# Eight projection products placed singly between the quarters of the scores and of the value pages, from the third sample on

## What is computed

```python
sb = jnp.einsum('bqhjd,bkhjd->bjhqk', qf, kb) - slopes[:, None, None] * d   # scores
pb = jnp.exp(sb - m_new[..., None])
acc = acc * corr[..., None] + jnp.einsum('bjhqk,bkhd->bjhqd', pb, vb)       # values
...
a = o[:, 0] - lam * o[:, 1]
mix = jnp.concatenate([a.reshape(B, S, ATT_W), s_out], axis=-1) @ w_out     # projection
x = x + ga1 * rms_norm(mix, g_post_mix)
```

## Time and profile before

| | us |
|---|---|
| median of 3 runs | 844.1 (839.42 to 849.49) |
| the profiled execution, its own time | 844.71 |
| span of the profile | 842.9 |
| time outside the span | 1.8 |
| mean granted clock of TensorE | 0.948 |

### The profile page before, as it was taken

One profiled execution on the slowest core, in us unless ns is written; L12 is line 12 of the kernel. 1 busy time (PEld: TensorE's weight loads), 2 busy tenths in 40 slices (PEclk: granted clock), 3 DMA queues, 4 the chain that ended last, 5 costly groups with the idle time before them and its releaser, 6 DMA issues.

```text
span 842.9 us, 12264 instructions
## 1 busy us (share of the span) xinstructions
PE 761.0 (90%) x5020; PEld 366.9 (44%) x5020; DVE 361.7 (43%) x830; ACT 184.0 (22%) x426; POOL 116.5 (14%) x169
## 2 busy tenths in 40 slices
PE   4699999999999839999999744999999999999994
PEld 3244343444444524545555333544444444444431
DVE  2212252536798846947665667100131011010146
ACT  4001000124454412413333211011011011110132
POOL 2220000200001111313221200100000000000054
PEclk9899999999999969979899965999999999999997
DMA  8979096580000996999999944788899999999793
GB/s 305 400 229 416 30 393 215 159 300 14 13 2 20 368 403 272 422 384 353 415 376 349 389 194 160 301 342 331 313 408 407 421 397 398 422 386 402 310 310 113
DMA packets 36602, 249.52 MB, mean 296 GB/s; under 512 B 4137, under 2 KB 5417, under 8 KB 23106
## 3 DMA queue, kind: packets, MB, share of 16 engines
q1 hardware_dynamic: 26482, 165.02, 50.5%
q0 software_dynamic: 9120, 81.34, 24.7%
q10 hardware_dynamic: 944, 2.38, 0.7%
HBM read 232.32 MB, written 16.40 MB: 295 GB/s over the span
## 4 chain that ended last, share of the span: by engine, by line
PE 74%; DMA 10%; DVE 9%; issue 2%; POOL 2%; SPq 2%; ACT 1%; POOLq 0%; DVEq 0%; ACTq 0%
PE ps L778 10%; PE ps L2454 8%; PE ps L2464 7%; PE ps L2489 7%; PE ps L1679 6%; PE ps L1069 5%; PE ps L2461 5%; PE ps L1597 4%; DMA sb<-in_w_ada 3%; PE ps L1647 3%; PE ps L2494 2%; DMA sb<-in_w_out 2%; PE ps L2426 2%; PE ps L535 2%; PE ps L1625 2%
## 5 line engine op out<-in xcount | busy, mean ns | idle before, releaser
L2464 PE MATMUL ps<-sb 128*128 128x512 f32 (+1 forms) x256 | 112.9, 594 | 0.0
L778 PE MATMUL ps<-sb 128*128 128x512 f32 x192 | 87.4, 610 | 1.4 <-DVE sb L436 1.4
L2388 DVE TENSOR_TENSOR sb<-sb,ps 128x512 f32<-128x512 f32 (+1 forms) x16 | 10.9, 684 | 160.4 <-PE ps L2464 94.7
L817 DVE STREAM_TRANSPOSE sb<-sb 128x1024 f32<-128x1024 f32 (+1 forms) x72 | 76.5, 1099 | 0.0
L2454 PE MATMUL ps<-sb 128*128 128x512 f32 x144 | 65.5, 608 | 1.0 <-ACT sb L2306 0.9
L2489 PE MATMUL ps<-sb 128*128 128x512 f32 x144 | 63.5, 594 | 0.0
L1679 PE MATMUL ps<-sb 128*128 128x512 f32 x128 | 61.9, 640 | 0.0
L1069 PE MATMUL ps<-sb 128*128 128x512 f32 x128 | 59.2, 597 | 0.3 <-DVE sb L972 0.3
L2464 PEld LDWEIGHTS ps<-sb 128*128 128x128 f32 (+1 forms) x256 | 42.0, 167 | 34.0 <-issue 34.0
L778 PEld LDWEIGHTS ps<-sb 128*128 128x128 f32 x192 | 36.5, 195 | 46.0 <-issue 42.9
L2461 PE MATMUL ps<-sb 128*64 128x512 f32 x112 | 49.6, 595 | 0.0
(11 more groups left out here) (347 smaller groups left out, 993.5 us busy)
## 6 DMA issues: line engine op xcount, KB each, us to landing
sb<-in_w_gate SPq DMA_DIRECT2D x16, 2048.0 KB, 19.0
sb<-in_w_up SPq DMA_DIRECT2D x16, 2048.0 KB, 9.9
sb<-in_w_down SPq DMA_DIRECT2D x16, 2048.0 KB, 14.4
sb<-in_w_ada SPq DMA_DIRECT2D x12, 2048.0 KB, 18.6
sb<-in_w_in SPq DMA_DIRECT2D x5, 2048.0 KB, 27.8
y_rows<-sb SPq DMA_DIRECT2D x9, 512.0 KB, 16.0
sb<-in_x_prompt SPq DMA_DIRECT2D x8, 512.0 KB, 6.7
sb<-in_w_out SPq DMA_DIRECT2D x2, 2048.0 KB, 20.6
```

Of the source, the lines that this page charges most:

```text
L778: last = pe.matmul(PS[:, n % 4, :], L.hT[:, k, t * P:t * P + P], w[:, k, :], start=k == 0, stop=k == KC - 1)
L817: dve.transpose(block, block).then_inc(self.turned, 1)
L2464: last = pe.matmul(PS[0:n, 1, :], x[:, k, :], w_up[:, k, :], start=k == 0, stop=k == KC - 1)
```

## The change

For samples 2 to 7 the eight products of `project_half(b)` are no longer a block between scores and values. `project_wait` (its waits: `mix_ev`, `wo_in`, `half_free`) goes ahead of the scores' own waits; product k = c stands behind quarter c of the scores, `s_done` goes up ahead of the fourth; products 4 to 7 stand behind each four pages of `values(f)`, `pv_half` goes up ahead of product 5. `logits`, where there are any, now stand between product 3 and the first pages. Turns 1 and 8 are as before. No product, wait or transfer is added or taken away.

```diff
             def scores(b, par):
+                if b >= 2:
+                    project_wait(b)
                 pe.wait_ge(turned, turned_to(b))
                 pe.wait_ge(q_st, b + 1)
...
                             last = pe.matmul(PS[32 * h:32 * h + 32, g, :], qst[par][r, h, 32 * c:32 * c + 32],
                                              kp[r, :, at_row:at_row + 32], start=c == 0, stop=c == 3)
-                last.then_inc(s_done, 1)
+                    if c == 3:
+                        last.then_inc(s_done, 1)
+                    if b >= 2:
+                        project_k(b, c)
...
-                    if half == 0:
-                        last.then_inc(pv_half, 1)
+                        if g == NPAGE // 2 - 1 and half == 0:
+                            last.then_inc(pv_half, 1)
+                        if g % 4 == 3 and 2 <= f + 1 < SB:
+                            project_k(f + 1, 4 + 2 * half + g // 4)
...
-            def project_half(u):
+            def project_wait(u):
...
+            def project_k(u, k):
+                last = pe.matmul(PS[:, 5, :], mixT(u // 2)[:, k, :], wo[u % 2][:, k, :], start=k == 0, stop=k == KC - 1)
+                if k == KC - 1:
+                    last.then_inc(half_done, 1)
+
+            def project_half(u):
+                project_wait(u)
                 for k in range(KC):
-                    last = pe.matmul(PS[:, 5, :], mixT(t)[:, k, :], wo[c][:, k, :], start=k == 0, stop=k == KC - 1)
-                last.then_inc(half_done, 1)
+                    project_k(u, k)
...
-                    project_half(b)
+                    if b == 1:
+                        project_half(b)
                 values(f)
```

## The result

| | before | after |
|---|---|---|
| median, us | 843.05 (22 runs, 838.23 to 849.49) | 848.42 (22 runs, 845.93 to 850.89) |
| ratio of the times | | 1.0069, 95% interval 1.0054 to 1.0084 |
| span of the profiled execution | 842.9 | 847.3 |
| its granted clock | 0.948 | 0.952 |

So 0.7% slower, within the 1% that was called "the same", at 848.4 where 849.0 was forecast. In the changed kernel's program the lines are L1599 (scores), L1688 (projection), L1652 (value pages), L1721 (logits), L1659 and L1753 (L1652 and L1738 of before).

What follows compares the result with a forecast made beforehand. PE, busy 90%, was taken to bound the kernel until the eighth `s_done`, then a transfer. Switches 8.5, waits 4.2, later signal 3.2 and gains -10.7 sum to +5.2 us; +5 on 844.1 gives 849, range 838 to 859.

Steps and rivals of the forecast that it cites:

- Part 1: PE, turns 2 to 7: entering and leaving single products and value pages costs 1.7 us a turn, 10.2 us in all.
- the switches hide: Rival on PE: switches between products and small tiles cost nothing, time 835 to 840 us; chance 0.15.
- Part 2: Ahead of the scores, the moved `half_free` wait holds PE 0.3 us in even and 1.1 in odd turns, 4.2 in all.
- Part 3: Scores of turns 3 and 5: both instruction-fetch gaps and the low clock behind them go, gaining 10.7 us.
- its yardstick, turn 7: Turn 7's scores, logits and product block, 13.7 us at full clock, served to price the gain in turns 3 and 5.
- with them what sets off the low clock: Turns 3 and 5: once the gaps go, the low clock goes too, some 8 us of the gain.
- Part 4: `s_done` comes three products, 3.2 us, later against the start of the scores; free for turns 2 to 6.
- For sample 7 it counts in full, as SyncE's loads hang on it.: At the eighth `s_done`, the 3.2 us later signal delays SyncE's loads and adds fully to the time.
- joins later and has some us of room: PE's path to the end of the last values, +3.7 us, was taken not to set the end.

Runs made afterwards that it cites:

- e2: Changed kernel with products 0 to 3 still singly between the score quarters, but 4 to 7 again one block behind the logits; 847.27 us, ratio 1.0037.
- e1: Changed kernel with `project_wait` moved from ahead of the scores to behind their first quarter; 845.70 us, ratio 1.0028.
- e4: Kernel before with 32 small products (128 PE records) added in PE's idle time ahead of turn 1; 841.98 us, one execution.
- e8: Kernel before with only 64 of 128 rows of each value page load moved for samples 2 to 7; 862.3 us, ratio 1.0219.
- e12: Changed kernel with scores in one piece, wait and products 0 to 3 as a block behind the logits, 4 to 7 still between value pages; 846.70 us, ratio 1.0040.
- e5: Kernel before, unchanged, in a second profiled execution; 844.38 us, one execution.
- e9: Kernel before with 48 small products (192 PE records) added in PE's idle time ahead of turn 1; 841.28 us, ratio 0.9978.
- e10: Changed kernel with turn 7 as in the kernel before, so that the eighth `s_done` comes early; 848.80 us, ratio 1.0072.
- e11: Changed kernel with the wait behind the first score quarter and products 4 to 7 as one block; 842.11 us, ratio 0.9995.
- e3: Kernel before with its block cut in two: wait and products 0 to 3 behind the second score quarter, 4 to 7 behind the logits; 844.85 us, ratio 1.0012.
- e7: Changed kernel with only 64 of 128 rows of each value page load moved for samples 2 to 7; 853.1 us, ratio 1.0108.

## Why the prediction was right, point by point

- **Part 1, switches.** Forecast 1.7 us a turn, measured 16.8 - 15.0 = 1.8, made of pieces as worked out (1.06 a product, 1.00 for four pages). A quarter and its product take 2.13 us (1.07 + 1.06), where 2.15 was said. Starts at the borders of other blocks carry over to single products. The rival "the switches hide" is out.
- **Part 2, the wait.** Forecast 0.3 and 1.1, 4.2 us in all; measured 0.41 to 0.44 and 1.19, 4.8 in all. The profile puts these pieces down to "issue", but ACT's copy ends 0.2 us before each of the two starts looked at (340.83 and 341.04, 362.81 and 363.01), and in e2 it names L1357 for the one of turn 3. e1 shows that the wait alone is some 3 us of the time.
- **Part 3, gaps and clock.** The cause of the gaps is shown (the packets ahead of all of them, e4, e8, e12), and that the breaks in the scores end them. By the PE stretch the gain was 6 x 1.8 + 4.8 - 3.1 = 12.5 us, against 10.7 forecast and 11.5 as its upper end. The term was undersized by its yardstick, turn 7: scores, logits and product block were taken as 13.7 us at full clock, but the clean pieces give 13.2 (4.39 + 1.77 + 7.06). That is 0.5 us too little in each of turns 3 and 5, and 0.7 in turn 7 itself, which was left out. The step "with them what sets off the low clock" was too simple: a gap is not enough for a fall (e4, e5, e9), a fall needs no gap (e4, turn 7), and 1.19 us of idle PE ahead of the scores are not enough either (after). What can be said is that without breaks in the scores the clock fell in the stretch in four profiles of five (before, e4, e5, e12; not e9), and with them and full page loads in none of six, one execution each. What sets it off is open. In 24 runs of the kernel before the time follows the mean clock (correlation -0.81, clocks 0.942 to 0.953), and in 22 of the changed kernel it does not (-0.11, 0.950 to 0.959); but in ten each of e1 and e2, whose clock does not fall in the stretch either, it does (-0.66, -0.74), so this says little about the stretch. The Trainium skill's sentence that fetching is hidden ("Runtime: NRT & Kernel Launch", Instruction fetch mechanics) does not hold here: in the two executions of the kernel before the gaps are 0.3 to 2.0 us long.
- **Part 4 and the sum.** The step that failed: "For sample 7 it counts in full, as SyncE's loads hang on it." The signal did come as late as worked out: 7.5 us later in the trace (452.8 to 460.3), 2.4 of which were there before turn 2 began; 5.1 remain, 5.2 were forecast. But from signal to landing the loads took 4.5 us less, where a few tenths to 1 us were forecast, and in e10 a signal 5.5 us earlier brought nothing. The other step that failed is that PE's path to the last values "joins later and has some us of room": it had about 2.4 us of room before (from L1652 at 465.9 on, plus the 5.9 us that the same way takes after the change, is 471.9, and L1993 started at 474.3), and after the change it is level with the loads and in the chain. Its end came 5.5 us later (466.2 to 471.7; 3.1 in the stretch, 2.4 ahead of it), the loads 3.0 (472.0 to 475.0). PE's path and the full DMA engines are both at the limit, and each takes a part of what the other gains.
- **The total.** +5 forecast, +5.4 measured (of medians). That it met so well is partly luck: it was added up at the eighth `s_done`, which does not set the end. And between the two profiles the times differ by 4.4 us, of which 3.0 stand at VectorE's finished rows and 1.4 come behind them; without those 2.4 us from ahead of turn 2 only 2 remain, while the medians differ by 5.4. The profiles of before (844.7 and 844.4) lie above its median, that of the changed kernel (849.1) does too. Single executions scatter by several us, and a sum made against one of them can't be held against a median to the us. How PE's 3.1 us and the later page loads (keys of sample 4 are issued at 349.0 instead of 342.9, 3.7 us later without the 2.4) share the 5.4 is open.

Of the versions tried e9 has the lowest median (841.28, ratio 0.9978), e11 equals the kernel before; no interval lies wholly below 1, so none is shown to beat it.

## What to carry to other kernels

Before an order is changed for the sake of one engine, look at the DMA share of the same stretch: at 0.96 there are only some us to be had, and e3, e11 and e9 show three different ways to a quicker PE that all stop there. Idle pieces that no semaphore ends, in the densest part of an unrolled program, can be instruction fetch: look whether an instruction packet stands at the same distance ahead of each, count records per packet, shift the program by half a packet, and see whether the gap moves. Ask at which point paths join, too: the sum here was made on a path that was no longer alone at the end. And where work is spread to break up such a stretch, spread it only there, and leave its wait where something covers it; here the breaks in the values and the moved wait were most of the cost (1.2 of 1.8 us a turn, and 4.8 us).

## What the runs showed of the hardware

- PE stood still for 0.3 to 2.0 us with full page traffic, and up to 4.9 with the half-row loads, in dense code: ahead of the first gap of the kernel before some 314 records (matmul and weight load) passed in 5.5 us (355.09 to 360.55), 58 a us. The queue brings a packet for every 250 or so of them.
- Each of the 16 gaps with full loads ended 2.2 to 2.6 us behind the point at which such a packet is counted (360.1 and 362.55 in turn 3 of the kernel before), each of the six in e7 and e8 2.7 to 3.0.
- A change between full 128x128 passes and tiled ones cost about 0.1 us on each side: a product alone takes 1.06 us among 32x32 or 128x32 tiles, where it takes 0.88 in a block (7.06 / 8). Four value pages alone take 1.00 us, where they take 0.90 in a row.
- Page loads of 64 rows instead of 128 halved the bytes of a load, but the DMA engines were still at a share of 0.84 with 235 GB/s in e8 and 0.94 with 279 in e7 (0.96 with 383 in the stretch of the kernel before), and the three kernels took 1.0 to 2.2% longer than the kernel before.
- The granted clock fell to 1.2 GHz for 10.2 us behind a gap of 2.0 us in one execution, and not at all behind the gap of 1.8 us at the same place in the next. It also fell for some 3 us in turn 7 of e4, where no gap stood ahead of it.
